# Input projection in three near-equal column groups, normalised columns handed over one at a time, mean square on VectorE, 1/rms spread by a repeated column

## The reference

```python
def rms_norm(x, g):
    xf = x.astype(jnp.float32)
    y = xf * lax.rsqrt(jnp.mean(xf * xf, axis=-1, keepdims=True) + EPS)
    return (y * g.astype(jnp.float32)).astype(x.dtype)

def swiglu(x, w_gate, w_up, w_down):
    return (jax.nn.silu(x @ w_gate) * (x @ w_up)) @ w_down

for l in range(DEPTH):            # DEPTH = 2
    x = x + 0.5 * swiglu(rms_norm(x, ffn1_norm[l]), ffn1_w_gate[l], ffn1_w_up[l], ffn1_w_down[l])
    h = rms_norm(x, mix_norm[l])
    proj = h @ w_in[l]
    qa, ka, va, c_q, c_kv, k_r, g_a, g_b = jnp.split(proj, IN_OFFSETS, axis=-1)
    ...
    o_a = swa_attention(qa, ka, va, ...)
    o_b = mla_attention(c_q, c_kv, k_r, ...)   # starts with rms_norm of c_q and of c_kv
    merged = jax.nn.sigmoid(g_a) * (o_a @ w_branch_a[l]) + jax.nn.sigmoid(g_b) * (o_b @ w_branch_b[l])
    x = x + merged @ w_out[l]
    x = x + 0.5 * swiglu(rms_norm(x, ffn2_norm[l]), ffn2_w_gate[l], ffn2_w_up[l], ffn2_w_down[l])
```

## Time and profile before

| | us |
|---|---|
| median of 3 timed runs | 1083.64 |
| lowest and highest of them | 1082.92, 1083.65 |
| the profiled execution, its own time | 1084.29 |
| its span in the trace | 1082.5 |
| PE busy | 1068.7 (99% of the span, 6240 matmuls) |
| DVE busy | 742.9 (69%) |
| ACT busy | 582.8 (54%) |
| POOL busy | 68.1 (6%) |

### The profile page before, as it was taken

One profiled execution on the slowest core, in us unless ns is written; L12 is line 12 of the kernel. 1 busy time (PEld: TensorE's weight loads), 2 busy tenths in 40 slices (PEclk: granted clock), 3 DMA queues, 4 the chain that ended last, 5 costly groups with the idle time before them and its releaser, 6 DMA issues.

```text
span 1082.5 us, 16614 instructions
## 1 busy us (share of the span) xinstructions
PE 1068.7 (99%) x6240; PEld 942.4 (87%) x6240; DVE 742.9 (69%) x1011; ACT 582.8 (54%) x912; POOL 68.1 (6%) x84
## 2 busy tenths in 40 slices
PE   8999999999999999999999999999999999999998
PEld 6888888899998888888888888888999988888887
DVE  5766666568887666666676666665788767666664
ACT  5555555455754645554565545544575547455543
POOL 3700000112000100000010000001220001000000
PEclk9999999999999999999999999999999999999999
DMA  7654553455334365544535545544363254455441
GB/s 276 216 191 175 200 207 139 135 174 196 119 128 152 112 224 187 206 188 174 193 148 218 200 174 180 206 146 150 129 217 134 85 189 165 184 185 211 185 174 58
DMA packets 35812, 187.60 MB, mean 173 GB/s; under 512 B 4528, under 2 KB 4672, under 8 KB 20672
## 3 DMA queue, kind: packets, MB, share of 16 engines
q1 hardware_dynamic: 35248, 186.52, 47.5%
q0 software_dynamic: 240, 0.53, 0.1%
q10 hardware_dynamic: 288, 0.05, 0.0%
HBM read 186.04 MB, written 1.05 MB: 173 GB/s over the span
## 4 chain that ended last, share of the span: by engine, by line
PE 94%; DVE 2%; DMA 1%; ACT 1%; issue 1%; POOL 0%; SPq 0%; DVEq 0%; ACTq 0%; POOLq 0%
PE ps L1185 91%; PE ps L1468 1%; DMA w_raw<-in_w_ffn 1%; DVE hT L846 1%; PE ps L1503 1%; ACT w_hi L501 1%; DMA x<-in_x 1%; ACT hT L554 0%; DVE w_lo L763 0%; PE ps L1493 0%; PE ps L1214 0%; DVE x L838 0%; PE ps L1388 0%; DVE w_lo L782 0%; POOL rs L420 0%
## 5 line engine op out<-in xcount | busy, mean ns | idle before, releaser
L1185 PE MATMUL ps<-hT,w_hi 128*128 128x512 f32 (+1 forms) x1920 | 449.6, 363 | 3.8 <-DVE hT L846 2.9
L1185 PEld LDWEIGHTS ps<-hT,w_hi 128*128 128x128 f32 x1920 | 336.9, 189 | 52.9 <-issue 4.0
L1185 PE MATMUL ps<-hT,w_lo 128*128 128x256 f32 x1664 | 272.9, 283 | 0.0
L1185 PEld LDWEIGHTS ps<-hT,w_lo 128*128 128x128 f32 x1664 | 245.0, 191 | 16.1
L763 DVE TENSOR_TENSOR w_lo<-w_raw,w_hi 128x2048 fp32r<-128x2048 f32 x83 | 190.2, 2292 | 76.3 <-ACT w_hi L501 76.3
L501 ACT ACTIVATE w_hi<-w_raw 128x2048 fp32r<-128x2048 f32 x86 | 164.3, 1911 | 19.4 <-PE ps L1185 14.1
L1185 PE MATMUL ps<-w_hi,aTh 128*128 128x512 f32 x352 | 138.3, 393 | 1.1 <-DVE aTl L822 1.1
L1185 PE MATMUL ps<-w_lo,aTh 128*128 128x512 f32 x352 | 138.1, 392 | 0.0
L1185 PE MATMUL ps<-w_hi,aTl 128*128 128x512 f32 x352 | 137.0, 389 | 0.0
L811 DVE TENSOR_TENSOR S<-ps,S 128x256 f32<-128x256 f32 x88 | 37.3, 424 | 142.0 <-ACT S L534 142.0
L757 DVE TENSOR_TENSOR w_lo<-w_raw,w_hi 128x2048 fp32r<-128x2048 f32 (+3 forms) x54 | 101.1, 1882 | 38.8 <-ACT w_hi L489 38.8
(11 more groups left out here) (162 smaller groups left out, 1062.7 us busy)
## 6 DMA issues: line engine op xcount, KB each, us to landing
w_raw<-in_w_ffn SPq DMA_DIRECT2D x86, 1024.0 KB, 5.4
w_raw<-in_w_ffn SPq DMA_DIRECT2D x90, 512.0 KB, 3.6
w_raw<-in_w_gate SPq DMA_DIRECT2D x16, 1024.0 KB, 4.9
w_raw<-in_w_proj SPq DMA_DIRECT2D x16, 592.0 KB, 3.9
w_raw<-in_w_branch SPq DMA_DIRECT2D x8, 1024.0 KB, 4.9
w_raw<-in_w_out SPq DMA_DIRECT2D x8, 1024.0 KB, 4.9
w_raw<-in_w_uq SPq DMA_DIRECT2D x4, 384.0 KB, 2.8
x<-in_x SPq DMA_DIRECT2D x2, 512.0 KB, 6.2
```

What stands on the lines that cost most here:

```text
L1185: return pe.matmul(dst, w, m, start=start, stop=stop, skip_group_check=True)
```

## The change

- **Projection:** column groups of 384, 384 and 416 instead of 512, 512 and 160, each in a bank of its own (`PROJ_GROUPS`, `PROJ_BANK`). ACT takes all six out of PSUM, c_q, c_kv and k_rope first; DVE takes none.
- **Columns:** PE, ACT and DVE signal after each chunk of 128 channels. Chunks 0 to 5 have a bank each; chunks 6 and 7 go to the other halves of the banks of chunks 0 and 1, so PE waits with their transposes until DVE is done with 0 and 1. The first feed-forward weight block is now gone through one chunk at a time.
- **Squares:** ACT makes three of the four, the last of these after all eight chunks; DVE makes the fourth after its chunks (`last_square`), in every norm.
- **Mean square:** the addition and mean + eps go from POOL to DVE (`mean_square`), ahead of the weight splits that follow there.
- **Spread:** no diagonals and no ones. PE uses the column rs, repeated 128 times by a step of zero, as weights and the identity as the moving operand: two float32 matmuls of 128 columns. In the mixing block the result lies in bank 2 instead of 3, and PE's wait for its copy moves ahead of gate block 1.
- **c_q and c_kv** are scaled by ACT, four instructions behind the split of gate block 3, instead of two on DVE.

```diff
-X_BANK = (2, 3, 4, 6)
-RS_BANK = (5, 3, 5)
-
-RS_STEPS = 4
+X_BANK = (2, 3, 4, 6, 5, 7, 2, 3)
+RS_BANK = (5, 2, 5)
+PROJ_GROUPS = ((0, 384), (384, 768), (768, PROJ_COLS))
+PROJ_BANK = ((4, 5, 1), (6, 7, 3))
+
+RS_STEPS = 2
...
-                pool.wait_ge(ss_done.sem, ss_done.at(l, 4 * n + 2 * TT - 1))
-                halves = ss[:, :].rearrange("p (t h) -> p t h", h=2)
-                then_rs(pool.tensor_tensor(rs_step[:, 0, :], halves[:, :, 0], halves[:, :, 1], ALU.add))
-                then_rs(pool.tensor_scalar(rs_step[:, 1, :], rs_step[:, 0, :], 1.0 / D_MODEL, EPS, ALU.mult, ALU.add))
+                pool.wait_ge(ms_var.sem, ms_var.at(l, n))
                 then_rs(pool.tensor_tensor(rs[:, :], rs_step[:, 1, :], minus_half[:, 0:TT], ALU.pow))
-                for t in range(TT):
-                    pool.tensor_scalar(diag[:, t, :], ident[:, :], rs[:, t:t + 1], None, ALU.mult).then_inc(diag_done.sem, 1)
                 then_rs(pool.tensor_scalar(half_rs[:, :], rs[:, :], 0.5, None, ALU.mult))
...
-                def columns_high(n, h, quarter=None):
+                def columns_high(n, part=range(KC)):
                     act.wait_ge(small_in.sem, small_in.per_layer * (l + 1))
-                    for c in range(4 * h, 4 * h + 4) if quarter is None else range(4 * h + 2 * quarter, 4 * h + 2 * quarter + 2):
-                        if c % 2 == 0:
-                            act.wait_ge(ht_ps.sem, ht_ps.at(l, 4 * n + c // 2))
-                        ins = act.activation(hTh[:, c, :], ps[:, X_BANK[c // 2], (c % 2) * SEQ:(c % 2 + 1) * SEQ], ACT.Copy,
-                                             scale=cols[:, 7 + n * KC + c:8 + n * KC + c])
-                        if c % 2:
-                            ins.then_inc(ht_hi.sem, 1)
+                    for c in part:
+                        act.wait_ge(ht_ps.sem, ht_ps.at(l, KC * n + c))
+                        act.activation(hTh[:, c, :], ps[:, X_BANK[c], c // 6 * SEQ:(c // 6 + 1) * SEQ], ACT.Copy,
+                                       scale=cols[:, 7 + n * KC + c:8 + n * KC + c]).then_inc(ht_hi.sem, 1)
 
                 def norm(n):
                     squares(n, 0)
-                    columns_high(n, 0)
-                    squares(n, 1)
-                    columns_high(n, 1)
+                    columns_high(n)
+                    squares(n, 1, (0,))
...
-                    act.activation(proj[:, t, HALF:2 * HALF], ps[:, 5 + 2 * t, :], ACT.Copy, scale=rs[:, t:t + 1])\
-                       .then_inc(proj_act.sem, 1)
...
+                for t, g in ((0, 2), (1, 2), (0, 0), (1, 0), (0, 1), (1, 1)):
+                    a, b = PROJ_GROUPS[g]
+                    act.activation(proj[:, t, a:b], ps[:, PROJ_BANK[t][g], 0:b - a], ACT.Copy, scale=rs[:, t:t + 1])\
                        .then_inc(proj_act.sem, 1)
...
+                act.wait_ge(c_rs.sem, c_rs.at(l, 0))
+                for a, b, r in ((CQ0, CKV0, 0), (CKV0, KR0, 2)):
+                    for t in range(TT):
+                        ins = act.activation(proj[:, t, a:b], proj[:, t, a:b], ACT.Copy, scale=rsC[:, r + t:r + t + 1])
+                ins.then_inc(c_norm.sem, 1)
...
-                def start_square(h):
+                def last_square(n, h=1):
 
                     part = x[:, 1, h * HALF:(h + 1) * HALF]
-                    dve.wait_ge(x_done.sem, x_done.at(0, h * TT + 1 - 2 * TT))
+                    dve.wait_ge(x_done.sem, x_done.at(l, 4 * n + h * TT + 1 - 2 * TT))
                     dve.scalar_tensor_tensor(out=sq[:, h * HALF:(h + 1) * HALF], in0=part, scalar=1.0, in1=part, op0=ALU.mult,
                                              op1=ALU.mult, accum_out=ss[:, 2 + h:3 + h]).then_inc(ss_done.sem, 1)
+
+                def mean_square(n):
+
+                    dve.wait_ge(ss_done.sem, ss_done.at(l, 4 * n + 2 * TT - 1))
+                    halves = ss[:, :].rearrange("p (t h) -> p t h", h=2)
+                    dve.tensor_tensor(rs_step[:, 0, :], halves[:, :, 0], halves[:, :, 1], ALU.add).then_inc(ms_sum.sem, 1)
+                    dve.wait_ge(ms_sum.sem, ms_sum.at(l, n))
+                    dve.tensor_scalar(rs_step[:, 1, :], rs_step[:, 0, :], 1.0 / D_MODEL, EPS, ALU.mult, ALU.add)\
+                       .then_inc(ms_var.sem, 1)
...
-                            dve.wait_ge(ht_hi.sem, ht_hi.at(l, 4 * n + c // 2))
-                        ins = dve.scalar_tensor_tensor(out=hTl[:, c, :], in0=ps[:, X_BANK[c // 2], (c % 2) * SEQ:(c % 2 + 1) * SEQ],
+                        dve.wait_ge(ht_hi.sem, ht_hi.at(l, KC * n + c))
+                        dve.scalar_tensor_tensor(out=hTl[:, c, :], in0=ps[:, X_BANK[c], c // 6 * SEQ:(c // 6 + 1) * SEQ],
                                                  scalar=cols[:, 7 + n * KC + c:8 + n * KC + c],
-                                                 in1=hTh[:, c, :].bitcast(F32), op0=ALU.mult, op1=ALU.subtract)
-                        if c % 2:
-                            ins.then_inc(ht_lo.sem, 1)
+                                                 in1=hTh[:, c, :].bitcast(F32), op0=ALU.mult, op1=ALU.subtract)\
+                           .then_inc(ht_lo.sem, 1)
...
                 columns_low(1)
+                last_square(1)
+                mean_square(1)
...
-                dve.wait_ge(rs_done.sem, rs_done.at(l, 2 * RS_STEPS - 1))
-                dve.wait_ge(gu_used.sem, gu_used.at(l, at_block("proj", KC - 1)))
-                for t in range(TT):
-                    dve.tensor_scalar(proj[:, t, CKV0:PROJ_COLS],
-                                      ps[:, 1, t * (KVRANK + ROPE):(t + 1) * (KVRANK + ROPE)], rs[:, t:t + 1], None, ALU.mult)\
-                       .then_inc(proj_dve.sem, 1)
-                dve.wait_ge(proj_dve.sem, proj_dve.at(l, TT - 1))
...
-                dve.wait_ge(c_rs.sem, c_rs.at(l, 0))
-                for a, b, r in ((CQ0, CKV0, 0), (CKV0, KR0, 2)):
-                    part = proj[:, :, a:b]
-                    ins = dve.tensor_tensor(part, part, rsC[:, r:r + 2].unsqueeze(2).to_broadcast([P, TT, b - a]), ALU.mult)
-                ins.then_inc(c_norm.sem, 1)
...
+                            if c >= 6:
+                                pe.wait_ge(ht_lo.sem, ht_lo.at(l, KC * n + c - 6))
                             for t in range(TT):
-                                ins = pe.transpose(ps[:, X_BANK[c // 2], (c % 2) * SEQ + t * P:(c % 2) * SEQ + (t + 1) * P],
+                                ins = pe.transpose(ps[:, X_BANK[c], c // 6 * SEQ + t * P:c // 6 * SEQ + (t + 1) * P],
                                                    x[:, t, c * P:(c + 1) * P], ident[:, :])
-                            if c % 2:
-                                ins.then_inc(ht_ps.sem, 1)
+                            ins.then_inc(ht_ps.sem, 1)
 
                 def spread_rs(n):
 
-                    pe.wait_ge(diag_done.sem, diag_done.at(l, TT * n + TT - 1))
-                    mm(ps[:, RS_BANK[n], 0:SEQ], ones[:, :], diag.rearrange("p t n -> p (t n)"), True, True).then_inc(rsb_ps.sem, 1)
+                    pe.wait_ge(rs_done.sem, rs_done.at(l, n * RS_STEPS))
+                    for t in range(TT):
+                        ins = mm(ps[:, RS_BANK[n], t * P:(t + 1) * P], rs[:, t:t + 1].to_broadcast([P, P]), ident[:, :], True, True)
+                    ins.then_inc(rsb_ps.sem, 1)
...
-                    for k0 in range(0, KC, 2):
-                        pe.wait_ge(ht_lo.sem, ht_lo.at(l, 8 * w + k0 // 2))
+                    for k in range(KC):
+                        pe.wait_ge(ht_lo.sem, ht_lo.at(l, 2 * w * KC + k))
+                        for s in range(2):
+                            c = (s * KC + k) * P
+                            high(s, wh_gu[0][:, c:c + P], k, k == 0)
                         for s, sig in enumerate((gate_ps, gu_used)):
-                            for k in (k0, k0 + 1):
-                                c = (s * KC + k) * P
-                                high(s, wh_gu[0][:, c:c + P], k, k == 0)
-                            for k in (k0, k0 + 1):
-                                c = (s * KC + k) * P
-                                ins = low(s, wl_gu[0][:, c:c + P], k, k == KC - 1)
+                            c = (s * KC + k) * P
+                            ins = low(s, wl_gu[0][:, c:c + P], k, k == KC - 1)
...
-                        for g, (a, b) in enumerate(((0, 512), (512, 1024), (1024, PROJ_COLS))):
-                            dst = ps[:, 4 + 2 * t + g, :] if g < 2 else ps[:, 1, t * (b - a):(t + 1) * (b - a)]
-
-                            ins = act_by_weight(dst, hTh[:, k, t * P:(t + 1) * P], hTl[:, k, t * P:(t + 1) * P],
-                                                hi[:, a:b], lo[:, a:b],
-                                                k == 0 and not (g == 2 and t == 1), k == KC - 1)
+                        for g, (a, b) in enumerate(PROJ_GROUPS):
+                            ins = act_by_weight(ps[:, PROJ_BANK[t][g], 0:b - a], hTh[:, k, t * P:(t + 1) * P],
```

(9 more changed lines are left out.)

42 lines of the change are left out of this document (18 added, 24 removed).

## The result

The changed kernel takes 1078.11 us (median of 5 runs, 1076.97 to 1078.45), against 1083.64 before. The ratio is 0.9949, 95% interval 0.9934 to 0.9964: 0.5% faster. Measured again in the first experiment it was 1078.34 against 1083.48. The forecast was 1077.3, the range 1075.4 to 1079.8. The profiled execution took 1078.45 with a span of 1076.6 us.

A forecast was written before the change was run, and what follows sets the result against it. PE, busy 1068.7 of 1082.5 us, was taken as the bound. Terms 3.5 + 2.1 + 0.7 = 6.3 us off 1084.29 gave 1078.0, or 1077.3 for the median; 8-in-10 range 1075.4 to 1079.8.

The forecast's parts named there:

- Widths: Projection: a token tile takes 1.60 us instead of 1.71, saving 3.5 us over 32 tiles; bounds 2.8 to 3.8.
- floor of 0.11 us: Projection: each 160-column matmul costs some 0.11 us, not its columns' 0.07; a 107 ns weight load taken as floor.
- upper bound of 3.8 us: Projection: most the widths could save, if 384 and 416 columns cost 2 ns less than the trace row.
- The rule that the cut of the columns is free: Projection: the skill's N/2.4 + 2.5 ns makes new widths worth 0, time 1080.8; rival's chance 0.08.
- Columns one by one: Five norms behind a residual: signalling after each chunk brings first products 0.43 us sooner, 2.1 us; bounds -1.0 to +3.7.
- The rival that the held queue gives the gain back: Norms: PE's in-order queue, held at chunks 6 and 7, cancels the earlier signal; 1079.4 us, chance 0.12.
- Squares and mean square on DVE: Norms: some 1.1 us added on DVE, offset by a 1.0 us hole; 0 us, or up to 1.1 lost each.
- The spread at the start: Program start: PE no longer waits for POOL's diagonals, saving 0.70 us; bounds 0 to 0.9.
- first-use penalty of 1 us: Program start: even with this extra on POOL's power, the result would be ready at 18.4 us.
- The operation itself: All six spreads: two float32 matmuls of 128 columns cost 0.44 us as before; 0 us, bounds -0.6 to +1.2.
- the PSUM reading: Projection: DVE's two instructions go, ACT's four become six of nearly the same columns; 0 us.
- A late weight load: Weight loads shift by microseconds, so a stall may go (1076.3 us) or a second come (1078.3); rival's chance 0.07.

The follow-up runs named there:

- the first experiment: The changed kernel measured again with no edit, in one job with the kernel before: 1078.34 us, ratio 0.9947.
- e1: Kernel before, with the new projection widths 384/384/416, ACT reading all six groups and the spread in bank 2: 1080.50 us, ratio 0.9974.
- e2: Changed kernel with the old projection widths 512/512/160, each group in its own bank and read by ACT: 1080.39 us, ratio 0.9967.
- e4: Changed kernel with projection groups of 512, 256 and 416 columns: 1077.34 us, ratio 0.9935.
- e3: Changed kernel with the columns handed over in pairs again, no wait ahead of chunks 6 and 7: 1080.09 us, ratio 0.9965.
- e10: Changed kernel with both second-half squares back on ScalarE between columns 3 and 4, none on VectorE: 1077.44 us, ratio 0.9944.
- e5: Changed kernel with sums, diagonals and the product with ones put back on POOL, the square staying on VectorE: 1087.67 us, ratio 1.0039.
- e0: The changed kernel again with no edit, for a second profile: 1078.34 us, ratio 0.9947.
- e8: e5 with VectorE's weight splits behind each feed-forward residual waiting for POOL's power: 1088.42 us, ratio 1.0047.

## Why the prediction was right

The mechanism and the sign were right, and the time came out 0.8 us above the forecast. By its steps:

- **Widths, forecast 3.5 us.** Right in kind, a quarter too large: 26.43 us for 26.0, 2.8 in both layers together, at the forecast's lower bound. The floor of 0.11 us for 160 columns is shown by e1, e2 and e4. The mis-sized term is the price of the wide groups: a tile takes 1.627 us, not 1.60. Steps of 384 lie 0.177 us apart and of 416 0.189, where the row taken from another product gave 0.173 and a line through it 0.187. (The upper bound of 3.8 us belongs to 1 ns less a matmul; 2 ns less, as the prediction has it, would be 4.1.) The rule that the cut of the columns is free, which the prediction set against the floor, would have left 27.8. No run varies the weight load, so that it sets the floor, as the prediction supposed, is not shown.
- **Columns one by one, forecast 2.1 us.** 0.48 a norm, 2.4 in sum, for 0.43. The chain is the predicted one: the first of chunk 7's transposes starts 1.98 us after the norm's first (forecast 2.08), the first product 2.18 (forecast 2.2), and PE waits for no later column. e3 gives all of it back, e10 keeps it without the squares. The rival that the held queue gives the gain back falls.
- **Squares and mean square on DVE, forecast 0.** The net is right, the account was incomplete. e10 shows the squares to be worth nothing. The sums' own cost is covered, but sums and diagonals are not free to be left on POOL once the last square is VectorE's: e5 puts the two together at 7.1 us from first transpose to spread, 9.3 between the medians. The prediction priced the delay on VectorE and never asked what stood beside POOL when its inputs come later.
- **The spread at the start, forecast 0.7 us.** 0.71 in e0 and 0.76 in the first profile, once the slow pace is taken off. That it is just 0.7 is in part luck: it hangs on PE's pace, and e1 waited 1.8 us there. The prediction gave no reason for POOL's 1.04, 1.04 and 1.60 us, and allowed for a first-use penalty of 1 us more. No run shows one: the times are not special to the start. e5 repeats them at 363 us beside splits, e8 removes them. The power takes 1.55 to 1.73 us in the changed kernel, in every norm, under cover. Since 1.6 was the value taken, the sum did not suffer.
- **The operation itself, and the PSUM reading, forecast 0.** A spread holds PE 0.36 us to the next start in the changed kernel; the stretch from spread to next norm behind it agrees with before to 0.01 us where no load stalls (177.64 in e0 and 177.65, layer 1's first feed-forward block).
- **A late weight load, a rival at 0.07.** It did move, down by 1.4 us in the first profile and by 0.6 in e0. It varies from run to run, and belongs in the range, not to the change.

The sum of what repeats is 2.8 + 2.4 + 0.7 = 5.9 us; the medians differ by 5.5 and 5.1. The remaining 0.4 to 0.8 is of the size of the stalls that come and go; which run has which is open, since only one of each is profiled. So the hit to 0.8 us rests on a right mechanism, and in part on errors that offset one another: 0.7 us too much for the widths, 0.3 too little for the columns.

## What to carry to other kernels

Where a matmul is too narrow to cover its floor (here 0.11 us), merge or widen the groups; equality of widths is worth nothing. When a chain hands over chunks through three engines, halve what the first signal waits for before touching the work behind it. Before moving a small operation onto or later on POOL, look at what VectorE does at that moment: with two inputs from SBUF it can make 0.2 us into 1.1, and 1.2 into 4.0. A wait of PE of 2 us may cost more than itself: look at the granted clock behind it (three of the six such waits in e5 and e8 were followed by 3.41 us at half clock, 1.7 us lost each).
